# Expert blocks of 1024 hidden columns, one PSUM bank for the scatter, and a sort in pieces

## The reference

```python
def moe_swiglu(xn, w_router, w_gate, w_up, w_down):
    logits = (xn @ w_router).astype(jnp.float32)
    top_v, top_i = lax.top_k(logits, TOP_K)
    top_w = jax.nn.softmax(top_v, axis=-1)
    gates = jnp.sum(jax.nn.one_hot(top_i, N_EXPERTS, dtype=jnp.float32) * top_w[..., None], axis=-2)
    out = jnp.zeros_like(xn)
    for e in range(N_EXPERTS):
        ye = swiglu(xn, w_gate[e], w_up[e], w_down[e])
        out = out + gates[..., e:e + 1].astype(xn.dtype) * ye
    return out
```

## Time and profile before

| | us |
|---|---|
| median of 3 runs | 1371.85 (1371.69 to 1371.88) |
| profiled execution, its own time | 1372.46 |
| profiled execution, span | 1370.7 |
| PE busy in the span | 1325.2 (97%) |
| DVE busy | 1154.4 (84%) |
| ACT busy | 951.4 (69%) |

### The profile page before, as it was taken

The page is one execution under the profiler, slowest core; times in us unless marked ns, Lnnn a source line. Parts: engine busy times, 40 slices in busy tenths (PEclk is TensorE's granted clock), DMA queues, the critical chain, the costliest instruction groups (busy, mean ns, idle before and its releaser), DMA issues.

```text
span 1370.7 us, 17261 instructions
## 1 busy us (share of the span) xinstructions
PE 1325.2 (97%) x6404; PEld 1083.2 (79%) x6404; DVE 1154.4 (84%) x970; ACT 951.4 (69%) x874; POOL 71.5 (5%) x110
## 2 busy tenths in 40 slices
PE   8999999999998999999999999999999999999998
PEld 7776888888886887777777767788888888888887
DVE  6897655557888989999999999998898899889886
ACT  5676544446775777777777777777777777776775
POOL 2120910000200000000000000000000000000000
PEclk9999999999999999999999999999999999999999
DMA  8743765555298989999999999999999999999980
GB/s 301 268 131 84 259 205 191 184 186 170 76 368 308 336 299 367 388 395 394 393 393 390 377 394 395 391 362 382 334 354 369 372 359 363 383 332 338 381 325 31
DMA packets 197860, 422.46 MB, mean 308 GB/s; under 512 B 13064, under 2 KB 37392, under 8 KB 197776
## 3 DMA queue, kind: packets, MB, share of 16 engines
q1 hardware_dynamic: 197776, 421.35, 85.1%
HBM read 420.27 MB, written 1.05 MB: 307 GB/s over the span
## 4 chain that ended last, share of the span: by engine, by line
PE 75%; DVE 16%; ACT 4%; issue 3%; SPq 1%; DMA 1%; POOL 0%; ACTq 0%; DVEq 0%; POOLq 0%
PE ps L334 20%; PE ps L336 19%; PE ps L335 19%; DVE w_lo L314 11%; PE ps L885 5%; ACT w_hi L297 3%; PE ps L883 3%; PE ps L1048 1%; PE ps L865 1%; PE ps L1023 1%; PE ps L1049 1%; PE ps L862 1%; PE ps L882 1%; DMA raw<-in_attn_w_qkv_dram 1%; DVE resid L2128 1%
## 5 line engine op out<-in xcount | busy, mean ns | idle before, releaser
L314 DVE TENSOR_TENSOR w_lo<-raw,w_hi 128x2048 fp32r<-128x2048 f32 x382 | 868.0, 2291 | 132.0 <-ACT w_hi L297 130.7
L297 ACT ACTIVATE w_hi<-raw 128x2048 fp32r<-128x2048 f32 x385 | 732.4, 1914 | 127.9 <-PE ps L336 105.5
L334 PE MATMUL ps<-w_hi,xe 128*128 128x512 f32 x448 | 179.2, 400 | 6.9 <-DVE w_lo L314 6.9
L336 PE MATMUL ps<-w_hi,xe 128*128 128x512 f32 x448 | 175.2, 391 | 0.0
L335 PE MATMUL ps<-w_lo,xe 128*128 128x512 f32 x448 | 175.2, 391 | 0.0
L334 PE MATMUL ps<-w_hi,h_t_hi 128*128 128x512 f32 x360 | 141.0, 392 | 0.3 <-DVE w_lo L314 0.3
L336 PE MATMUL ps<-w_hi,h_t_lo 128*128 128x512 f32 x360 | 140.3, 390 | 0.0
L335 PE MATMUL ps<-w_lo,h_t_hi 128*128 128x512 f32 x360 | 140.1, 389 | 0.0
L334 PE MATMUL ps<-w_hi,xb 128*128 128x512 f32 x280 | 111.5, 398 | 1.9 <-DVE w_lo L314 1.9
L885 PE MATMUL ps<-a_all,w_hi 128*128 128x512 f32 x308 | 109.8, 396 | 0.0
L336 PE MATMUL ps<-w_hi,xb 128*128 128x512 f32 x280 | 109.2, 390 | 0.0
(11 more groups left out here) (319 smaller groups left out, 1854.2 us busy)
## 6 DMA issues: line engine op xcount, KB each, us to landing
raw<-in_moe_w_gate_dram SPq DMA_DIRECT2D x112, 1024.0 KB, 7.8
raw<-in_moe_w_up_dram SPq DMA_DIRECT2D x111, 1024.0 KB, 7.9
raw<-in_moe_w_down_dram SPq DMA_DIRECT2D x111, 1024.0 KB, 7.5
raw<-in_attn_w_qkv_dram SPq DMA_DIRECT2D x11, 1024.0 KB, 12.3
raw<-in_ffn_w_gate_dram SPq DMA_DIRECT2D x11, 1024.0 KB, 5.3
raw<-in_ffn_w_up_dram SPq DMA_DIRECT2D x11, 1024.0 KB, 5.4
raw<-in_ffn_w_down_dram SPq DMA_DIRECT2D x11, 1024.0 KB, 4.9
raw<-in_ple_w_gate_dram SPq DMA_DIRECT2D x8, 1024.0 KB, 7.0
```

What stands on the lines that cost most here:

```text
L297: nc.scalar.activation(w_hi[:, u % SPLIT, :], raw_slot(u), ACT.Copy).then_inc(hi_ready, 1)
L314: nc.vector.tensor_tensor(w_lo[:, u % SPLIT, :], raw_slot(u), w_hi[:, u % SPLIT, :].bitcast(F32), ALU.subtract).then_inc(lo_ready, 1)
L334: nc.tensor.matmul(out, x[0], w[0], start=first, stop=False)
L336: return nc.tensor.matmul(out, x[1], w[0], start=False, stop=last)
```

## The change

- The hidden columns go in blocks of 1024 (`BLOCKS = 4`, the last one has 512). A wide block has four gate units, four up units (2 chunks by 1024 columns each) and the down units of the block before; the narrow block keeps units of 4 chunks by 512. A turn still has 42 units. Gate sums stand in banks 0 and 1, up sums in 6 and 7; silu and the product with up take 1024 columns at a time.
- The hidden block is turned in two halves, behind the first gate unit and the first up unit of the next block, and ACT and DVE split the halves at places named in their loops.
- Scatter pieces all use bank 5, each behind a gate or up unit of block 1 (`SCATTER_AT`), and every one but the first waits for the addition of the one before. DVE's additions stand behind its splits of fixed units (`ADD_AT`).
- The pick matrix is turned in bank 5 and copied by ACT.
- The gather goes in four pieces, each ahead of one down unit of the last block, in banks 1, 5, 7, 5.
- The sort works in other buffers (`qk_gain`, `rope`), without waiting for the split of the token rows, and is cut in two parts (`sort_experts`, `place_experts`) in block 1 of turn 0; the two splits of the rows stand in that block too, each by itself.

```diff
+BLOCKS = 4
+BLOCK_AT = (0, 10, 22, 34)
+HALVES = (2, 2, 2, 1)
...
+                for b in range(BLOCKS):
+                    views = []
+                    for w in (ge, ue):
+                        n0, n = 1024 * b, 512 * HALVES[b]
+                        chunk = 4 // HALVES[b]
+                        views += [expert_rows(w, e, c0, chunk, n0, n) for c0 in range(0, KD, chunk)]
+                    if b or not first:
+                        before_it = (b - 1) % BLOCKS
+                        views += [expert_rows(de, e if b else e_before, 8 * before_it + 2 * j, 2, 0, D)
+                                  for j in range(2 * HALVES[before_it])]
...
+        PIECE_BANKS = (1, 5, 7, 5)
...
-                if q < 2 and t % 2 == 0:
-                    pe.wait_ge(xe_lo_ready, 2 * (t + 3 + k))
-                elif q < 2:
-                    pe.wait_ge(added, 4 * (t + k))
-                else:
-                    pe.wait_ge(added, 4 * (t + k) + q - 1)
+                if q:
+                    pe.wait_ge(added, 4 * (t + k) + q)
                 tt, half = q // 2, q % 2
                 for y, stop in ((y_hi, False), (y_lo, True)):
-                    last = nc.tensor.matmul(ps[:, 5 + q % 2, :], pick_t[:, tt * P:(tt + 1) * P],
+                    last = nc.tensor.matmul(ps[:, 5, :], pick_t[:, tt * P:(tt + 1) * P],
...
+            def gate_or_up(t0, b, n, i, k=0, few=False):
+                x, width = xb if t0 == 2 else xe, 512 * HALVES[b]
+                chunks = 4 // HALVES[b]
+                u = block_unit(t0, b) + n * KD // chunks + i
+                unit(u, k)
+                if b == 0 and n == 0 and t0 < 2:
+                    pe.wait_ge(xe_lo_ready, 2 * (t0 + k) + (i + 1 if t0 else i // 2 + 1))
+                if i == 0:
+                    pe.wait_ge((silu_ready, hidden_ready)[n], JF + BLOCKS * t0 + b + BLOCKS * k)
+                for c in range(chunks):
+                    d = chunks * i + c
+                    for half in range(HALVES[b]):
+                        out, w = ps[:, 6 * n + half, :], weights(u, c, 512 * half, 512, width)
+                        first, stop = d == 0, d == KD - 1
+                        if few and n == 1:
+                            last = product_few(out, x[:, 2 * d * P + FEW:2 * d * P + FEW + P], w, first, stop)
+                        else:
+                            last = product(out, (x[:, 2 * d * P:(2 * d + 1) * P], x[:, (2 * d + 1) * P:(2 * d + 2) * P]), w,
+                                           first, stop)
+                last.then_inc(unit_used, 1)
...
+                for b in range(BLOCKS):
+                    units = 2 * HALVES[b]
+                    before_it, t_before = (b - 1) % BLOCKS, t0 if b else t0 - 1
+                    few_then = few if b else few_before
+                    late = t0 == 0 and b == 1
+                    for n in range(2):
+                        for i in range(units):
+                            gate_or_up(t0, b, n, i, k, few)
+                            if (n, i) == ((0, 2) if late else (0, 0)) and (t0 or b):
+                                transpose_hidden(t_before, before_it, 0, k, few_then)
+                            if (n, i) == ((1, 1) if late else (1, 0)) and (t0 or b) and HALVES[before_it] == 2:
+                                transpose_hidden(t_before, before_it, 1, k, few_then)
+                            if b == 1 and t0 and (n, i) in SCATTER_AT:
+                                scatter(SCATTER_AT.index((n, i)), t0 - 1, k)
+                            if b == 2 and (n, i) == (0, 1):
+                                transpose_picks(t0, k)
+                    if b == 1 and t0:
+                        pe.wait_ge(y_lo_ready, t0 + k)
+                    if b or t0:
+                        u = block_unit(t0, b) + 2 * units
+                        for j in range(2 * HALVES[before_it]):
+                            if b == BLOCKS - 1 and t0 != 1:
+                                gather_piece(j, t0, k)
+                            down(u + j, before_it, j, half_at(t_before, before_it), k, few=few_then)
+                            if end and b == BLOCKS - 1 and j == 1:
+                                transpose_hidden(t0, b, 0, k)
+            SCATTER_AT = ((0, 2), (0, 3), (1, 1), (1, 2))
...
+                    wide, wide_before = HALVES[b] == 2, HALVES[before_it] == 2
+                    for n in range(0 if b or t0 else 1, 2 * units + (2 * HALVES[before_it] if b or t0 else 0)):
                         split_lo(u + n + AHEAD, k)
+                        if n == 1 and b == 1 and t0:
+                            result_lo(t0 - 1, k)
+                        if n == (3 if late else 1) and (t0 or b):
+                            hidden_lo(t_before, before_it, 0, k, few_then)
+                        if n == ((7 if late else 6) if wide else 4) and (t0 or b) and wide_before:
+                            hidden_lo(t_before, before_it, 1, k, few_then)
+                        if n == ((8 if t0 or b else 7) if wide else 4):
+                            hiddens(t0, b, k)
+                        if b == 1 and t0 and n in ADD_AT:
+                            add_result(ADD_AT.index(n), t0 - 1, k)
+                        if late and n == 2:
                             sort_experts()
+                        if late and n == 5:
+                            place_experts()
+                        if late and n in (9, 11):
+                            rows_lo_of((n - 9) // 2)
+                        if b == 2 and n == 5 and t0 != 1:
+                            dve.wait_ge(pick_transposed, t0 + 1 + k)
+                            picks(t0 + 1, 0, k, few=few_next[0])
+                            picks(t0 + 2, 1, k, few=few_next[1])
+                        if b == BLOCKS - 1 and t0 != 1 and n >= 4:
+                            piece_lo(n - 4, t0, k)
+                        if end and b == BLOCKS - 1 and n == 6:
+                            hidden_lo(t0, b, 0, k, to=(a_hi[:, 0:512], a_lo[:, 0:512]))
+            ADD_AT = (3, 4, 6, 7)
...
+                    wide, wide_before = HALVES[b] == 2, HALVES[before_it] == 2
+                    for n in range(0 if b or t0 else 1, 2 * units + (2 * HALVES[before_it] if b or t0 else 0)):
+                        split_hi(u + n + AHEAD, k)
+                        if n == 0 and b == 1 and t0:
+                            result_hi(u - 1, k)
+                        if n == (3 if late else 1) and (t0 or b):
+                            hidden_hi(t_before, before_it, 0, k, few_then)
+                        if n == (4 if wide else 2):
+                            silus(t0, b, k)
+                        if n == ((7 if late else 6) if wide else 4) and (t0 or b) and wide_before:
+                            hidden_hi(t_before, before_it, 1, k, few_then)
+                        if b == 2 and n == 3:
+                            copy_pick(t0, k)
+                        if b == BLOCKS - 1 and t0 != 1 and n >= 4:
+                            piece_hi(n - 4, t0, k, few_next)
+                        if end and b == BLOCKS - 1 and n == 6:
+                            hidden_hi(t0, b, 0, k, to=a_hi[:, 0:512])
```

More of the change, by code:

```diff
@@ L1026, in gather_pair @@
                                                 start=rows is a_hi and tt == 0, stop=rows is a_lo and tt == 1)
-                    if c % 2:
-                        last.then_inc(gathered, 1)
+                last.then_inc(gathered, 1)
             def scatter(q, t, k=0):
@@ L1066, in down @@
                 last.then_inc(unit_used, 1)
-            def turn(t0, k=0, end=False, few=False, few_before=False):
[L1070 to L1119, removed]
@@ L1136, in _ @@
             for half in range(2):
-                down(U_TURN + half, FB - 1, half, JF + FB - 1, turns, end=half == 1, h_t=(a_hi, a_lo))
+                down(U_TURN + half, BLOCKS - 1, half, JF + FB - 1, turns, end=half == 1, h_t=[(a_hi, a_lo)])
             def last_scatter(n, tt):
@@ new lines, in turn @@
+            def turn(t0, k=0, end=False, few=False, few_before=False, few_next=(False, False)):
+                for b in range(BLOCKS):
+                    u, units = block_unit(t0, b), 2 * HALVES[b]
+                    before_it, t_before = (b - 1) % BLOCKS, t0 if b else t0 - 1
+                    few_then = few if b else few_before
+                    late = t0 == 0 and b == 1
+                    wide, wide_before = HALVES[b] == 2, HALVES[before_it] == 2
[15 more added lines that the diff above has]
+                            hidden_hi(t0, b, 0, k, to=a_hi[:, 0:512])
@@ L1534, in _ @@
                 nc.scalar.activation(a_hi[:, tt * D:(tt + 1) * D], xs[:, tt, :], ACT.Copy).then_inc(rows_split_hi, 1)
-            turn(0)
+            turn(0, few_next=(True, True))
             act.wait_ge(more_ready, 1)
@@ L1540, in _ @@
             turn(1, 0, few=True)
-            turn(2, 0, few=True)
-            turn(1, 2, few=True)
-            turn(2, 2)
```

(28 more changed lines are left out.)

236 lines of the change are left out of this document (95 added, 141 removed).

## The result

The changed kernel takes 1416.65 us (median of 6 runs, 1413.86 to 1419.77) against 1372.52 for the kernel before in the same measurement: ratio 1.0321, 95% interval 1.0308 to 1.0335, so +44 us where +28 was forecast. The profiled execution's span is 1414.1 us, 43.4 more than before. Its runs also differ more from each other than those of before do (5.9 us between the ends, 2.0 before).

What follows compares the result with a forecast made beforehand. PE bounds full turns; in few turns PE, ACT and DVE hang in a ring of three buffers. Terms +32.4 - 4.8 - 1.4 + 2.1 = +28.3 on 1372.46 gave 1400.8, stated as 1400 us; range 1384 to 1422.

Steps and rivals of the forecast that it cites:

- main case: Whole kernel: the summed terms give 1400 us, between 1385 and 1412, chance 0.59.
- the rival of the falling clock: PE's clock falls to half at the new gaps: +24 us at all 14, +8 at a third; over 1412, chance 0.20.
- waits for additions: Turns 1 to 7: PE waits for DVE's additions before the second and fourth scatter pieces, +32.4 us.
- turn 0: Cutting the sort in pieces leaves PE gaps of 2.4 us in place of 7.2 us lost: gain 4.8 us.
- wide blocks, gather: Blocks of 1024 cost few turns +2.1 us; the gather in four pieces removes turn 2's gap, -1.4 us.
- The round of the ring: In the three-buffer ring, DVE's split of unit u+3 ends at the earliest 4.44 us after PE finishes unit u.
- The bank rule: Independent matmul groups should rotate through PSUM banks; alone it prices the scatter's wait at 0.7 us, hidden: +0.
- The signs: Right: 2 to 3 us scatter gaps, turns near 115 and 125 us; wrong: no gap, half clock in every turn.
- the run of four gate units: Few turns: three buffers can't level it, so DVE idles about 1.6 us there; wide blocks cost +2.1 in all.
- the scatter waits hide: Rival: DVE's split is done when PE reaches piece 1, no waits; 1368.4 us, down to 1356; chance 0.10.
- the few turns win: Rival: without ACT's own waits DVE runs through in three few turns, 12.4 us less, 1374.5 us; chance 0.08.

Runs made afterwards that it cites:

- small matmuls in the gaps: Changed kernel with 28 small matmuls, values never read, ahead of the waits of the second and fourth scatter piece: 1402.29 us, ratio 1.0220.
- earlier additions: Changed kernel with each of DVE's four additions one split earlier (ADD_AT 2, 3, 5, 6): 1369.93 us, ratio 0.9977; measured again, 1370.11 us, ratio 0.9984.
- kernel before with the pieces alone: Kernel before with only the sort's buffers changed, the sort in two pieces and the row splits moved: 1367.07 us, ratio 0.9963.

## Why the prediction was right, and where a term was off

The time lies in the range and the waits are the forecast ones. But it lies above the main case (1385 to 1412, chance 0.59), and in the range because that had been drawn to take in the rival of the falling clock.

| Term | forecast, us | measured, us | from |
|---|---|---|---|
| waits for additions | +32.4 | +32.4 | small matmuls in the gaps less earlier additions |
| clock at the gaps | 0 in the sum, +8 to +24 as a rival | +13.9 | changed kernel less small matmuls in the gaps |
| turn 0 | -4.8 | -5.0 | kernel before with the pieces alone |
| wide blocks, gather (measured: and all else that differs) | +0.7 | +3.0 | earlier additions against the pieces alone |
| all | +28.3 | +44.1 | |

The measured terms come from three measurements and add up to 44.3. The same kernel with earlier additions was 3.2 us faster than the kernel before in one measurement and 2.0 in another, so the sum closes no better than to a microsecond or two.

**Which wait.** The four gaps of a pair of turns were forecast as 2.2 and 3.2 (few), 2.2 and 2.6 (full). They measure 1.93 and 3.20, and 1.98 and 2.37; the first full turn has 2.26 and 2.53. The whole of it is 33.2 us on one line of the trace. The round of the ring, 4.44 us from the earlier trace rows, is what carried this. That +32.4 came out to the tenth is luck: the forecast was 35.4 us of gaps less 3.0 that few turns give back, the measurement 33.2 of gaps and hardly anything given back.

**The bank rule.** The rule of the Trainium skill (Perfetto Trace Analysis, Matmuls) names the remedy rightly: with pieces in three banks the gaps are gone. The price that the prediction worked out for it taken alone, nothing, was wrong for this order, where the waits cost 32.4 us, and right for the order with the addition one split earlier, where a single bank costs nothing. With one bank, what decides is what stands ahead of the evacuation in DVE's queue, not the evacuation.

**The step that was off** is the clock. The sum left it out and gave a chance of 0.20 to its moving the time over 1412; it did. The prediction had a row on its side, the fall 2.05 us into a gap, and gaps of 2.0 to 3.2 beside it. Of the fourteen falls that the rival priced at 1.7 each, eight came, 13.6 by that price, and 13.9 us is the measured cost. The size is partly luck: two of the eight lasted 6.83 us and not 3.4, and half of the 34.1 us at half clock would be 17. The right sum had the clock in. It goes with the scatter of the runs too: the six runs have mean clocks from 0.991 (1413.86 us, the fastest) down to 0.984 (1419.77 us, the slowest). Not every gap of the same length brings a fall: the gap of 1.98 at 1028.10 did, that of 1.98 at 1156.03 did not, and one of 1.93 us in turn 2 did where the next, of 3.17, did not.

**The signs.** One that was to show the prediction wrong did come: a half clock in every turn. Two of the right ones failed by the same step: PE's busy time in the full turn rose by 3.6 us, and the turns without gather take 118.3 and 119.7 (few) and 127.9 us (full) where 115 and 125 were named. With the clock held up they take 116.0, 117.5 and 124.75.

**Turn 0.** The forecast left 2.4 us of gaps; there are 0.90 and 0.28. DVE's lead there is 2.0 us, not the 1.0 worked out: the sort proper holds up the splits for 2.95 us and PE waits 0.90, and with the sort in one piece it is 6.80 (from 413.22 to 420.02) and 4.76.

**Wide blocks.** In the first few turn before, ACT waited 9.8 us for hidden blocks, 5.1 for silu and 11.7 for buffers, 26.6 in all; with earlier additions it waits 26.8 us, all for buffers. The waits for silu and hidden blocks went, as the prediction says, but waits for buffers took their place. DVE's idle time in that turn rose from 7.0 to 8.7 us (14 waits for ACT, the longest 1.0).

That the run of four gate units is the reason fits these numbers but was not tried by itself. Turn by turn, earlier additions against the pieces alone, the three few turns differ by +1.3, -0.1 and +2.8 us and the three full ones by +0.5, -0.4 and -0.3: it is the few turns that lose, and more than the +2.1 forecast. Some of it is what is left of the scatter waits (0.5 us a few turn). Of the gather's gap of 1.46 us in turn 2, 0.54 is still there, so about 0.9 of the 1.4 forecast was won, and the whole turn is only 0.1 shorter than in the kernel before (115.05 against 115.18).

**The rivals.** That the scatter waits hide, and that the few turns win, are both out: no gap hid, and few turns are 5.6 to 9.0 us longer with the gaps and 0 to 3 without. The loads are not a bound, before or after: nobody waits for one. With wide pieces the queue's share in the first few turn is 1.01 with earlier additions, where the turn is about as long as before, against 1.03; the 0.98 of the changed kernel has the longer turn in it.

## What to carry to other kernels

Where engines run in a ring of few buffers, give each step that another engine waits for a place counted in the ring's round: what stands behind the split of unit u+3 can't be had before unit u is used, plus one round (4.44 us here). One place earlier or later in a hand-written order was worth 47 us. Look at every new gap of PE for what the clock adds, and if a gap can't go, fill it.

## What the runs showed of the hardware

- Gaps of 1.93 to 3.20 us on PE in otherwise dense work were followed by half clock (1.2 GHz) in eight of fourteen cases, and each fall lasted 3.41 or 6.83 us. The length alone didn't decide: one of 1.93 us brought a fall and one of 3.17 none. Gaps of 0.79 us between small matmuls and scatter (and 1.53 in the few turns) brought none, nor did one of 1.54 in turn 0.
- 28 matmuls of 128 bf16 columns, 1.74 us of otherwise idle time, ahead of each of the fourteen waits left the clock at 1.0, and were worth 13.9 us over seven turns.
